# One gate-product step moved ahead of the score-value products, and their wait split in two

## The chip, the cores and the metric

The kernel runs on one core of one Trainium2 chip. The metric is the device time of the whole program in microseconds (us), all stages from the first load to the last store; lower is better. Every number below comes from the kernel before the change: three timed runs and one profiled execution.

## What is computed

One step of a hybrid decoder layer over 1024 prompt tokens and 8 x 4 sample tokens (1056 in all), model width 1024. The part that matters here is gated linear attention in chunks and the branch gates:

```
proj = rms_norm(x) @ w_in            # GLU input, q, k, v, output gate r, low-rank forget gate, gate_c, gate_g
# per chunk of tokens and head; b = cumulative log forget gate inside the chunk
o     = (q * exp(b)) @ s  +  att @ v          # att[t,s] = sum_k q[t,k] k[s,k] exp(b[t,k]-b[s,k]), s <= t
s_new = exp(b_last) * s   +  (k * exp(b_last - b)).T @ v
o     = rms_norm(o) * gla_norm * silu(r)
h     = x + (sigmoid(gate_c) * conv_out + sigmoid(gate_g) * (o @ w_gla_out)) @ w_out
out   = h + hierarchical_moe(rms_norm(h))     # 4 groups x 8 experts, top 2
```

Heads: 4, with 128 key and 256 value channels each.

## The kernel before, in words

The instruction stream of each engine is written out by hand, in the order in which it runs; engines wait for each other through counting semaphores (`wait_ge`, `then_inc`). The stages are: the input projection by slabs of 512 columns, with every weight and activation split into a high and a low part (three matmuls replace one); the causal convolution; **the chunk stage**; the sample tokens with the convolution's output product; the product with `w_gla_out`; `w_out` and routing; the experts; the last norm.

The chunk stage has 8 chunks of 128 tokens. In each, TensorE runs two independent kinds of work, interleaved by hand:

- **Gate products** (`gate_block`, L1148). Per chunk 2 column blocks of the gates (k = 0, 1) times 3 thirds of the tokens (j = 0 to 2). One product is 8 steps over the contraction (`parts`), and one step is three matmuls with 352 columns: `nTH,gateH`, `nTL,gateH`, `nTH,gateL`. All six have L999 as their line, the helper that records a matmul. Products (k, j) are numbered g = 3k + j and alternate between PSUM banks 0 and 1 (`bk[g % 2]`). Before the first step of a product TensorE waits until ScalarE has taken the product that was two numbers earlier (L1151). ScalarE takes a product by writing it to `stage` (`gate_out`).
- **The attention of the chunk** (`chunk`, L1158). First 9 "levels" (LV = 7): seven small products of decayed queries and keys (`gwork`), the diagonal product (`qkbuf`, l = 7), and the transposes of the decayed keys `kdT` (L1177, l = 8), each in bank 2 or 3. Behind each of the first eight levels stands one step of gate product (1, 0). VectorE takes each level out of PSUM: levels 0 to 7 are copied under masks into the scores `attn` (L2127, L2134), level 8 into the turned keys `kdn` (L2139). Each taking raises `lev_taken` by one; it starts at 2.
- Then come the **score-value products** (`vrbuf,attn` and `state,qe`, four heads, banks 4 and 5), which raise `o_ready`; then the **state products** (`vrbuf,kdn`, banks 6 and 7), which raise `ds_ready`; then gate products (1, 1) and (1, 2); a drain; and the transposes of the normed output `onorm` (L1204).

Beside this VectorE updates `state` after `ds_ready` (L2085), forms `onorm` (L2095), and prepares the next chunk (`prepare`, L1889). ScalarE squares the outputs after `o_ready`, takes gate product (1, 0), computes the exponentials of the next chunk (`factors`), and takes gate products (1, 1) and (1, 2) in the midst of those. SyncE loads the next chunk's inputs and gate columns when `oT_ready` and `gw_free` allow it, and after the last chunk the states and the weights of the convolution's output product (`cw_raw`). GpSimd only stores `stage` here.

The wait ahead of the score-value products stands at L1184: it asks for `lev_taken` to be `c * (LV + 2) + (LV + 4)`, which is all nine levels of the chunk, `kdn` among them.

Of the kernel before, what the change touches and what calls it, by code (L numbers as in the profile page):

```python
# [39 lines left out]
def hybrid_layer(nc, a, o):  # L40
# [13 lines left out]
    KC = D // P  # L54
# [5 lines left out]
    LV = 7  # L60
# [28 lines left out]
    with ctx:  # L89
# [3 lines left out]
        def sem(name):  # L93
            return ctx.enter_context(nc.semaphore(name))
# [208 lines left out]
        lev_taken = sem("lev_taken")  # L303
# [250 lines left out]
        def third(j):  # L554
            return slice(j * BLK, (j + 1) * BLK)
# [441 lines left out]
        def _(pe):  # L997
            def mm(out, lhsT, rhs, start, stop, **kw):
                return pe.matmul(out, lhsT=lhsT, rhs=rhs, start=start, stop=stop, **kw)  # L999
# [24 lines left out]
            def by_token(out, wh, wl, t0, parts=range(KC)):  # L1024
                for k in parts:
                    last = three(out, wh(k), wl(k), nTH[:, k, t0], nTL[:, k, t0], k == 0, k == KC - 1)
                return last
# [35 lines left out]
            for n in range(1, 1 + H + CC):  # L1063
# [4 lines left out]
                else:  # L1068
                    c = B_JOB.index(n)
# [37 lines left out]
            for m in range(VRJ):  # L1107
# [15 lines left out]
                if m in LN_JOB:  # L1123

                    j = LN_JOB.index(m)
# [9 lines left out]
                if m - 1 in LN_JOB:  # L1135

                    j = LN_JOB.index(m - 1)
# [10 lines left out]
            def gate_block(c, b, k, j, parts=range(KC)):  # L1148
                g = k * 3 + j
                if parts[0] == 0:  # L1150
                    pe.wait_ge(gate_taken, c * 6 + (g + 1))  # L1151
                    if j == 0:
                        pe.wait_ge(low_made, c * 2 + (N_SLAB + k + 1))
                last = by_token(bk[g % 2][:, 0:BLK], lambda q: gateH[k][:, q, :], lambda q: gateL[2 * b + k][:, q, :],
                                third(j), parts)
                if parts[-1] == KC - 1:
                    last.then_inc(gate_ready, 1)

            def chunk(c, b, i):
                for j in range(3):  # L1160
                    gate_block(c, b, 0, j)
                pe.wait_ge(prep_made, c + 1)
                lv = lev.rearrange("p l (h t) -> p l h t", h=H)
                for l in range(LV + 2):
                    x = (LV + 2) * b + l
                    pe.wait_ge(lev_taken, c * (LV + 2) + (l + 1))
                    dst = bk[2 + x % 2]
                    for h in range(H):
                        if l < LV:
                            m = 64 >> l  # L1170
                            right = lv[:, l, h, :].rearrange("p (n z i) -> p n z i", z=2, i=m)[:, :, 1, :]
                            last = mm(dst[:, 64 * h:64 * h + 64].rearrange("p (n i) -> p n i", i=m),
                                      lv[:, l, h, :], right, True, True)
                        elif l == LV:
                            last = mm(dst[:, P * h:P * h + P], qkb[b][:, 1, h, :], qkb[b][:, 0, h, :], True, True)
                        else:
                            last = pe.transpose(dst[:, P * h:P * h + P], kdT[:, h, :], ident[:, :])  # L1177
                    last.then_inc(lev_ready, 1)

                    if l < KC:  # L1180
                        gate_block(c, b, 1, 0, [l])

                pe.wait_ge(oT_taken, c + 1)
                pe.wait_ge(lev_taken, c * (LV + 2) + (LV + 4))  # L1184
                pe.wait_ge(s_made, c + 1)
                pe.wait_ge(vc_loaded[b], i * 16 + 16)
                for h in range(H):
                    dst = bk[4 + h // 2][:, DV * (h % 2):DV * (h % 2 + 1)]
                    mm(dst, attn[:, h, :], vch[b][:, h * DV:(h + 1) * DV], True, False)
                    last = mm(dst, qe[:, h, :], state[:, h, :], False, True)  # L1190
                last.then_inc(o_ready, 1)
                for h in range(H):
                    last = mm(bk[6 + h // 2][:, DV * (h % 2):DV * (h % 2 + 1)], kdn[:, h * P:(h + 1) * P],
                              vch[b][:, h * DV:(h + 1) * DV], True, True)
                last.then_inc(ds_ready, 1)
                for j in range(1, 3):
                    gate_block(c, b, 1, j)
                pe.drain().then_inc(gw_free, 1)
                o_transposes(P, c + 1)

            def o_transposes(r, wait):
                pe.wait_ge(on_made, wait)
                for k in range(KC):
                    last = pe.transpose(bk[4 + k // 4][:, P * (k % 4):P * (k % 4) + r],  # L1204
                                        onorm[0:r, k * P:(k + 1) * P], ident[0:r, 0:r])
                last.then_inc(oT_ready, 1)

            with pe.Fori(0, NCH // 2) as i:
                for b in range(2):
                    chunk(i * 2 + b, b, i)  # L1210
# [1286 lines left out]
```

## Time and profile before

| what | value |
|---|---|
| timed runs | 1838.51, 1838.77, 1839.8 us; median 1838.77 |
| profiled execution, own time | 1836.5 us |
| its span | 1834.9 us |
| mean granted TensorE clock | 0.97 of full speed |
| busy share of the span: TensorE, VectorE, ScalarE | 93%, 68%, 50% |
| HBM traffic | 324.35 MB read, 61.22 MB written |
| chunk stage (first gate product to last transposes) | about 470 to 780 us in the trace |

The profile gives busy time per engine, the chain of work that ended last, waits by who was waited for, and a timeline with the start of each instruction in us from the start of the span. PE is TensorE's matmul queue, PEld its weight loads, DVE VectorE, ACT ScalarE, POOL GpSimd, SP SyncE. Ends of matmuls are modelled and overlap the next start, so distances are best read from start to start.

### The profile page before, as it was taken

How to read it: one execution, taken by the hardware profiler on the slowest of the kernel's cores; microseconds unless marked ns; L12 is line 12 of the kernel's file. 1: busy time of each engine (PE TensorE's matmuls, PEld its weight loads, DVE VectorE, ACT ScalarE, POOL GpSimd, SP SyncE). 2: the span in 40 equal slices, each digit the busy share in tenths (PEclk: the TensorE clock that was granted, in tenths of full speed). 3: DMA queues.
4: the chain of work that ended last, by engine and by line, in shares of the span. 5: the costliest groups of instructions: out<-in, count | busy, mean ns of one | idle time of the engine just before them, and what ended most of it. 6: DMA issues, size and time to landing. Idle time of an engine off the chain costs nothing.

```text
span 1834.9 us, 24415 instructions
## 1 busy us (share of the span) xinstructions
PE 1710.3 (93%) x8996; PEld 1494.0 (81%) x8996; DVE 1239.1 (68%) x2000; ACT 913.8 (50%) x1085; POOL 226.4 (12%) x260
## 2 busy tenths in 40 slices
PE   6999989999899999989998996999999999999981
PEld 5999978777899999958997885788888888877771
DVE  5243789962566565653444556988989888888873
ACT  5262021114443333323433343787878877787763
POOL 3100111000000000001000123211111112221210
PEclk9999999999999999989999997999999999999995
DMA  4401222231124322153534327899999999999955
GB/s 172 139 36 59 70 93 100 88 107 38 65 87 137 123 86 86 43 197 98 183 120 161 104 88 264 321 360 376 364 384 383 383 392 388 377 375 376 359 204 194
DMA packets 101645, 366.18 MB, mean 200 GB/s; under 512 B 14389, under 2 KB 55569, under 8 KB 87744
## 3 DMA queue, kind: packets, MB, share of 16 engines
q1 hardware_dynamic: 78864, 308.06, 45.1%
q0 software_dynamic: 22704, 57.12, 9.7%
q8 instruction: 45, 0.74, 0.2%
q14 instruction: 32, 0.26, 0.0%
HBM read 324.35 MB, written 61.22 MB: 210 GB/s over the span
## 4 chain that ended last, share of the span: by engine, by line
PE 80%; DMA 6%; PEld 5%; DVE 4%; ACT 2%; issue 2%; DVEq 0%; PEldq 0%; SPq 0%; ACTq 0%; POOLq 0%
PE bank L999 77%; PEld bank L999 5%; DMA wraw_down<-in_w_expert_down 3%; PE bank L1401 2%; DMA wraw_gate<-in_w_expert_gate 1%; PE bank L1422 1%; DVE fbuf L2468 1%; DMA uo<-in_x_prompt 1%; DVE wL_gate L1889 0%; PE bank L1325 0%; PE bank L1204 0%; DMA stage<-xn_scr,kdT 0%; DMA h_scr<-ybuf,kdT 0%; DVE attn L2134 0%; DVE woL L1889 0%
## 5 line engine op out<-in xcount | busy, mean ns | idle before, releaser
L1889 DVE TENSOR_TENSOR wL_down<-wraw_down,wH_down 128x2048 fp32r<-128x2048 f32 x72 | 161.8, 2288 | 58.6 <-ACT wH_down L1490 58.6
L1889 DVE TENSOR_TENSOR wL_up<-wraw_up,wH_up 128x2048 fp32r<-128x2048 f32 x72 | 161.5, 2284 | 15.9 <-ACT wH_up L1490 15.9
L1889 DVE TENSOR_TENSOR wL_gate<-wraw_gate,wH_gate 128x2048 fp32r<-128x2048 f32 x72 | 161.6, 2286 | 6.3 <-ACT wH_gate L1490 6.1
L1490 ACT ACTIVATE wH_up<-wraw_up 128x2048 fp32r<-128x2048 f32 x72 | 134.1, 1910 | 59.2 <-DMA wraw_up<-in_w_expert_up 43.2
L1490 ACT ACTIVATE stage<-bank 128x512 f32<-128x512 f32 (+4 forms) x63 | 33.4, 546 | 255.3 <-PE bank L999 255.3
L2010 DVE SCALAR_TENSOR_TENSOR ybuf<-uo,gwork,ybuf 128x1024 f32<-128x1024 f32 x120 | 153.6, 1280 | 6.1 <-issue 6.1
L1490 ACT ACTIVATE wH_down<-wraw_down 128x2048 fp32r<-128x2048 f32 x72 | 133.8, 1910 | 12.8 <-DMA wraw_down<-in_w_expert_down 12.6
L999 PE MATMUL bank<-nTH,gateH 128*128 128x352 f32 x384 | 132.5, 345 | 5.3 <-DVE gateL L1889 5.3
L1490 ACT ACTIVATE wH_gate<-wraw_gate 128x2048 fp32r<-128x2048 f32 x72 | 134.2, 1923 | 2.6 <-DMA wraw_gate<-in_w_expert_gate 2.4
L999 PE MATMUL bank<-nTH,slabH 128*128 128x352 f32 x384 | 127.0, 331 | 5.9 <-DVE nTL L1889 5.6
L999 PE MATMUL bank<-nTL,slabH 128*128 128x352 f32 x384 | 124.9, 325 | 0.0
L999 PE MATMUL bank<-nTH,slabL 128*128 128x352 f32 x384 | 124.7, 325 | 0.0
L999 PE MATMUL bank<-nTL,gateH 128*128 128x352 f32 x384 | 124.2, 324 | 0.0
L999 PE MATMUL bank<-nTH,gateL 128*128 128x352 f32 x384 | 124.2, 323 | 0.0
L999 PE MATMUL bank<-wH_down,hidTH 128*128 128x512 f32 x288 | 113.7, 395 | 10.6 <-DVE hidTL L1889 10.6
L999 PE MATMUL bank<-slabH,nTH 128*128 128x512 f32 x288 | 116.8, 406 | 5.5 <-DVE slabL L1889 4.7
L943 POOL DMA_INDIRECT h_scr<-ybuf,kdT x36 | 67.5, 1875 | 433.6 <-ACT ybuf L1490 393.4
L999 PE MATMUL bank<-wH_gate,xeH 128*128 128x512 f32 x288 | 114.3, 397 | 6.4 <-DVE wL_gate L1889 3.8
L999 PE MATMUL bank<-wH_up,xeH 128*128 128x512 f32 x288 | 115.9, 402 | 0.0
L999 PE MATMUL bank<-slabH,nTL 128*128 128x512 f32 x288 | 114.3, 397 | 0.0
L999 PE MATMUL bank<-slabL,nTH 128*128 128x512 f32 x288 | 114.1, 396 | 0.0
L999 PE MATMUL bank<-wH_gate,xeL 128*128 128x512 f32 x288 | 113.5, 394 | 0.0
(309 smaller groups left out, 4297.2 us busy)
## 6 DMA issues: line engine op xcount, KB each, us to landing
wraw_gate<-in_w_expert_gate SPq DMA_DIRECT2D x36, 2048.0 KB, 14.9
wraw_up<-in_w_expert_up SPq DMA_DIRECT2D x36, 2048.0 KB
wraw_down<-in_w_expert_down SPq DMA_DIRECT2D x36, 2048.0 KB
slab_raw<-in_w_in SPq DMA_DIRECT2D x8, 2048.0 KB, 8.4
gate_scr<-stage POOLq DMA_DIRECT2D x16, 528.0 KB, 3.6
vr_scr<-stage POOLq DMA_DIRECT2D x32, 256.0 KB, 2.3
gate_raw<-in_w_in SPq DMA_DIRECT2D x16, 512.0 KB, 8.0
vrbuf<-vr_scr SPq DMA_DIRECT2D x16, 512.0 KB, 6.2
```

What stands on the lines that cost most here:

```text
L943: pool.indirect_dma_start(out=h_scr, in_=yo[n % 2], in_offset=None, out_offset=bass.IndirectOffsetOnAxis(ap=lst_tok[:, n:n + 1], axis=0), ...
L999: return pe.matmul(out, lhsT=lhsT, rhs=rhs, start=start, stop=stop, **kw)
L1401: last = pe.transpose(bk[k // 4][:, P * (k % 4):P * (k % 4 + 1)], xg[b][:, k:D:KC], ident[:, :])
L1422: last = pe.transpose(bk[4][:, P * k:P * (k + 1)], hid[:, k:DE:FC], ident[:, :])
L1490: return act.activation(out, in_, func, **kw)
L1889: return dve.tensor_tensor(out, x, y, op)
L2010: dve.scalar_tensor_tensor(ybuf[:, c, 0:SEQ], u[:, c, bass.ds(w, SEQ)], tap, ybuf[:, c, 0:SEQ], ALU.mult, ALU.add)
L2468: dve.scalar_tensor_tensor(fo[t][0:r, :], fh[t][0:r, :], rstd9[t][0:r, :], nfin[0:r, :], ALU.mult, ALU.mult).then_inc(f_made, 1)
```

## The change

In `chunk` of TensorE's program:

```diff
                     if l < KC:
                         gate_block(c, b, 1, 0, [l])
 
+                gate_block(c, b, 1, 1, [0])
                 pe.wait_ge(oT_taken, c + 1)
-                pe.wait_ge(lev_taken, c * (LV + 2) + (LV + 4))
+                pe.wait_ge(lev_taken, c * (LV + 2) + (LV + 3))
                 pe.wait_ge(s_made, c + 1)
                 pe.wait_ge(vc_loaded[b], i * 16 + 16)
                 for h in range(H):
@@
                 last.then_inc(o_ready, 1)
+                pe.wait_ge(lev_taken, c * (LV + 2) + (LV + 4))
                 for h in range(H):
                     last = mm(bk[6 + h // 2][:, DV * (h % 2):DV * (h % 2 + 1)], kdn[:, h * P:(h + 1) * P],
                               vch[b][:, h * DV:(h + 1) * DV], True, True)
                 last.then_inc(ds_ready, 1)
-                for j in range(1, 3):
-                    gate_block(c, b, 1, j)
+                gate_block(c, b, 1, 1, range(1, KC))
+                gate_block(c, b, 1, 2)
                 pe.drain().then_inc(gw_free, 1)
                 o_transposes(P, c + 1)
```

The score-value products now wait for eight levels, the state products for the ninth. The first step of gate product (1, 1) is issued ahead of both, the other seven remain behind them. No arithmetic changes, and no engine but TensorE has another order.

TensorE's order at the front of the score-value products, first chunk of the loop body; `kdT` is what the transposes read, `gateH_85` and `gateL_81` are the gate columns of block k = 1:

```order
 L1177 MATMUL bank<-ident,kdT 128x128 x4
-L1184 REGISTER_ALU
-L1186 ISA
+L1151 REGISTER_ALU
+L999 MATMUL bank<-nTH,gateH_85 128x352
+L999 MATMUL bank<-nTL,gateH_85 128x352
+L999 MATMUL bank<-nTH,gateL_81 128x352
+L1185 REGISTER_ALU
+L1187 ISA
 L999 MATMUL bank<-vrbuf,attn 128x256
```

Three matmuls now stand between the key transposes and the first score-value product, where there was only the wait.

The same engine behind the last score-value product; `kdn` is read by the state products:

```order
 L999 MATMUL bank<-state,qe 128x256
+L1193 REGISTER_ALU
 L999 MATMUL bank<-vrbuf,kdn 128x256 x4
-L1151 REGISTER_ALU
-L999 MATMUL bank<-nTH,gateH_85 128x352
-L999 MATMUL bank<-nTL,gateH_85 128x352
-L999 MATMUL bank<-nTH,gateL_81 128x352
```

A wait has come in ahead of the state products, and three of the 24 matmuls of gate product (1, 1) have left from behind them.

## Rows read from the trace of the kernel before

**Rows 1.** The page, busy time: us, share of the span, instructions.
```profile
PE 1710.3 (93%) x8996; PEld 1494.0 (81%) x8996; DVE 1239.1 (68%) x2000; ACT 913.8 (50%) x1085; POOL 226.4 (12%) x260
```
**Rows 2.** The page, chain that ended last, shares by engine.
```profile
PE 80%; DMA 6%; PEld 5%; DVE 4%; ACT 2%; issue 2%; DVEq 0%; PEldq 0%; SPq 0%; ACTq 0%; POOLq 0%
```
**Rows 3.** That chain in the chunk stage: start us, length us, what.
```profile
588.21 22.00 PE bank L999 x157
...
611.44 0.70 DVE kdn L2139
612.15 0.04 issue
612.19 13.15 PE bank L999 x72
...
650.55 0.12 issue
```
**Rows 4.** Waits of TensorE, 480 to 790 us: total us, times, longest.
```profile
PE bank L999 <- DVE kdn L2139: 9.1, 8, 1.2
```
**Rows 5.** Timeline, TensorE, end of one chunk's levels: start us, us, engine, line, what.
```profile
609.96 0.41 PE L999 MATMUL bank<-nTH,gateH 128*128 128x352 f32 x1
...
610.21 0.32 PE L999 MATMUL bank<-nTL,gateH 128*128 128x352 f32 x1
610.21 0.19 PEld L999 LDWEIGHTS bank<-nTH,gateL 128*128 128x128 f32 x1
...
610.36 0.32 PE L999 MATMUL bank<-nTH,gateL 128*128 128x352 f32 x1
...
610.52 0.60 PE L1177 MATMUL bank<-ident,kdT 128*128 128x128 f32 x4
...
612.19 0.70 PE L999 MATMUL bank<-vrbuf,attn 128*128 128x256 f32 x2 [1.07 <-DVE kdn L2139]
...
612.73 0.59 PE L999 MATMUL bank<-state,qe 128*128 128x256 f32 x2
...
613.16 0.59 PE L999 MATMUL bank<-vrbuf,attn 128*128 128x256 f32 x2
...
615.75 1.89 PE L999 MATMUL bank<-vrbuf,kdn 128*128 128x256 f32 x8
...
621.34 0.32 PE L999 MATMUL bank<-nTH,gateH 128*128 128x352 f32 x1
```
**Rows 6.** Timeline, VectorE, the same chunk: the last masked copy of the scores.
```profile
610.35 0.89 DVE L2134 COPY_PREDICATED attn<-masks,bank 128x128 f32<-128x128 int8 x4 [0.70 <-PE bank L999]
```
**Rows 7.** Timeline, TensorE, output transposes and the next chunk's first gate product.
```profile
625.45 1.09 PE L1204 MATMUL bank<-ident,onorm 128*128 128x128 f32 x8
...
626.30 0.41 PE L999 MATMUL bank<-nTH,gateH 128*128 128x352 f32 x1
```
**Rows 8.** Timeline, ScalarE, the same chunk: squares, gate products (1, 0) and (1, 1) taken.
```profile
615.95 0.38 ACT L1490 ACTIVATE gwork<-bank 128x256 f32<-128x256 f32 x1 [14.65 <-PE bank L999]
...
619.07 0.54 ACT L1490 ACTIVATE stage<-bank,par 128x352 f32<-128x352 f32 x1
...
624.93 0.54 ACT L1490 ACTIVATE stage<-bank,par 128x352 f32<-128x352 f32 x1
```
**Rows 9.** By stretch: us, busy PE, PEld, DVE, ACT, POOL, granted clock, DMA, GB/s.
```profile
610.00:648.30 38.30, 37.12 (x247) 35.96 (x246) 24.28 (x77) 14.36 (x28) 1.06 (x2) 1.00 0.33 104
...
795.00:800.00 5.00, 5.00 (x13) 2.43 (x13) 2.74 (x5) 3.40 (x7) 0.00 (x0) 0.50 0.42 97
...
1130.00:1500.00 370.00, 361.67 (x1697) 302.68 (x1698) 326.06 (x220) 292.88 (x244) 63.25 (x44) 0.98 0.97 368
```
**Rows 10.** Timeline behind the last chunk: last gate product taken (ScalarE), convolution weights issued (SyncE).
```profile
778.72 0.55 ACT L1490 ACTIVATE stage<-bank,par 128x352 f32<-128x352 f32 x1 [3.26 <-PE bank L999]
...
782.72 1.52 SPq L665 DMA_DIRECT2D cw_raw<-in_w_conv_out  x1
```
**Rows 11.** DMA issues, 470 to 800 us: KB each, us to landing.
```profile
cw_raw<-in_w_conv_out SPq DMA_DIRECT2D x1, 2048.0 KB, 13.8
```

## The prediction

> **What bounds the kernel now.** I began with the busy times: TensorE is at work 93% of the span, VectorE 68%, ScalarE 50% [rows 1]. The chain that ended last says the same: TensorE's matmuls make 80% of it [rows 2]. So what counts is time in which TensorE stands still, or work that it needn't do. The change touches the chunk stage alone, so I read the chain there [rows 3]. It is a plain alternation: 22.00 us of matmuls, then a hand-over through VectorE that ends in the copy of the turned keys (0.70 us) and an issue gap of 0.04 us (0.12 us in every second chunk), then 13.15 us of matmuls. The list of TensorE's waits gives the size of that hand-over: eight waits for the `kdn` copy, 9.1 us in all, 1.14 us each [rows 4]. Nothing else repeats in TensorE's waits there. The clock is granted in full in a whole chunk [rows 9], so matmul times can be taken as they stand.
>
> The timeline shows what the wait is for. The four key transposes start at 610.52; the first score-value product starts at 612.19 [rows 5]. Its operands `attn` were complete at 610.35 + 0.89 = 611.24 [rows 6]. What TensorE really stood for was the copy that ended at 611.44 + 0.70 = 612.14 [rows 3], and only the state products at 615.75 [rows 5] need that one.
>
> **The change part by part.**
>
> *The wait on the scores instead of the turned keys.* Between the start of the transposes and the first score-value product lie 612.19 - 610.52 = 1.67 us in this chunk, where the idle time is 1.07 us; with the mean idle of 1.14 us it is 1.74 us per chunk.
>
> *The step put in front.* When can it start? Eight transposes take 1.09 us and the next gate matmul starts 626.30 - 625.45 = 0.85 us after their start [rows 7]; four take 0.60 us [rows 5], 0.49 less, so the step should start 0.36 us after the transposes do. A step behind attention work lasts 610.52 - 609.96 = 0.56 us from start to start (0.25 + 0.15 + 0.16) [rows 5]. So the score-value products could start 0.36 + 0.56 = 0.92 us after the transposes, at 611.44 in this chunk. The scores are released at 611.24 plus the 0.04 to 0.12 us of issue [rows 3, 6], that is by 611.36. So the new wait is just covered by the moved step, with about 0.1 us to spare: front part 1.74 - 0.92 = **0.82 us saved** per chunk.
>
> *The step taken away from behind.* Three matmuls, 0.16 us from start to start each (the third in rows 5: 610.52 - 610.36), are gone from gate product (1, 1): **0.48 us saved**. The cold start behind the state products stays, it falls on the next step.
>
> *The start of the score-value products.* After the idle time the first group took 612.73 - 612.19 = 0.54 us, the next 613.16 - 612.73 = 0.43 [rows 5]. If weights are loaded ahead, 0.11 us goes too. Between 0 and 0.11 us; I count none of it, because TensorE can load ahead only in the 0.1 us by which the scores are early.
>
> *The second wait, ahead of the state products.* By the sum they start at about 611.44 + (615.75 - 612.19) = 615.0 [rows 5], and `kdn` is there at 612.14: 2.9 us of cover, cost nothing. What stands behind the wait on TensorE are the state products, for which VectorE waits, and the gate products. If that cover were gone, TensorE would wait for the rest of a 0.70 us copy.
>
> *The open group in bank 0.* Its first step needs gate product (0, 2) taken, which ScalarE did long before; SyncE's and GpSimd's queues are moved past nothing, and their issues follow TensorE's semaphores.
>
> Sum per chunk: 0.82 + 0.48 = 1.30 us, times 8 chunks = **10.4 us**. The bounds: 1.41 us with the start-up gained (11.3 us in all), and 1.14 us (9.1 us) if the weights of the first score-value product aren't loaded during the moved step: 0.16 us until its last matmul has ended, rather than started its successor.
>
> A rule of the Trainium skill prices the moved matmuls otherwise. The rows give 0.16 us from start to start for 352 columns. The page "TensorE: Matmul & The Clock Gate", section "Back-to-back issue gap", gives N/2.4 + 2.5 ns, which is 149 ns, an estimate, and no extra for following other work. By it the step costs 0.45 us in front and saves 0.45 us behind, 1.38 us per chunk and 11.0 us in all. I keep the rows' 0.56 and 0.48.
>
> **What is late next.** Everything downstream of the score-value products on VectorE and ScalarE moves up by 0.82 us, TensorE's own later work by 1.30 us, so all slacks against ScalarE shrink by 0.48 us. The nearest: the next chunk's first gate product uses bank 0 and needs product (1, 1) taken. Taken at 624.93 + 0.54 = 625.47 [rows 8], needed at 626.30 [rows 7]: 0.83 us of slack, 0.35 us left. Product (1, 0) was taken at 619.07 + 0.54 = 619.61 [rows 8] and is needed at 621.34 [rows 5]: 1.73, then 1.25 us. Both hold.
>
> **Does it reach the end?** The chunks' end releases all that follows: ScalarE takes the last gate product right behind TensorE [rows 10], and the convolution weights are issued only when the last chunk has freed their buffer and land 13.8 us later [rows 10, 11]. Loads with fixed durations therefore shift with the chunks. The profiled execution took 1836.5 us; the sum makes it 1826.1. It lies 2.3 us under the median of the timed runs, so I take the 10.4 us from the median: 1838.77 - 10.4 = **1828.4 us**, a ratio of 0.9943. A measurement of this kernel can tell about 0.2% from no change, 3.7 us.
>
> **The rivals.**
>
> *Weights aren't loaded ahead.* The trace shows the load of the next weights at 610.21 under a matmul that runs from 609.96 for 0.41 us [rows 5], which speaks against it. Price as worked out: 1.14 us per chunk, 9.1 us, 1829.7 us. The same page of the Trainium skill says in its Part 3, "What overlaps and what doesn't", that a weight load overlaps a running matmul only in another row group; here the row group is the same, and that row disagrees.
>
> *ScalarE becomes the next wait.* If the taking of product (1, 1) doesn't move up with `o_ready`, because its exponentials are held by something else, TensorE wants bank 0 at 626.30 - 1.30 = 625.00 and gets it at 625.47 + 0.1: 0.57 us lost at seven hand-overs, 4.0 us. The gain is 6.4 us: 1832.4 us. For it: the slack is only 0.35 us. Against it: squares, root, norm and differences all start from `o_ready` and `ds_ready`.
>
> *The gain is swallowed later.* In the expert stage the DMA engines are busy 0.97 of the time [rows 9]. If the stream of expert weights set the end and didn't start earlier, nothing would be left: 1838.8 us. Against it: the stream starts on buffers that TensorE's products free.
>
> *The clock turns it round.* After the last chunk TensorE idles and runs at half clock (0.50 in the stretch from 795 to 800 us, 1.2 instead of 2.4 GHz) until the convolution products have run for a while [rows 9]. Such stretches may fall otherwise when everything shifts. Work at full clock done at half clock costs its own duration again; if 15 us of the convolution or expert products fell into such a stretch anew, the loss is 15 us against the gain of 10.4: 1843.4 us. It decides the sign from 10.4 us of such work on. Against it: the stretch before is short, and the idle time that leads to it is the same after the change.
>
> *The change doesn't do what it says*: the scores may be released later than thought, so that the wait remains in part. Since the scores' copy ends 0.90 us before the keys' copy, at the very least the step behind and most of this are gained; the result is one of the times above.
>
> **How the numbers follow.** Forecast (9.8 to 11.3 us gained) 0.65; weights not ahead 0.12; ScalarE late 0.11; swallowed 0.05; clock 0.03. 0.04 is left for larger gains, where a stretch at half clock gets shorter by some us. The range for 8 in 10 reaches from 1825.5 (13 us gained) to 1832.8 (6 us gained), which takes in the first three cases with about 1 us of scatter, as the timed runs show. Faster by over 0.2%: 0.92; within 0.2%: 0.05; slower by over 0.2%: 0.03.
>
> **What would show it.** Right: in the chunk stage the eight waits for `kdn` are gone, the distance from the key transposes to the first score-value product is 0.9 to 1.0 us with three gate matmuls in it, and a chunk lasts 37.0 instead of 38.3 us. ScalarE's row of taking product (1, 1) ends 0.3 us before the next chunk's first gate matmul. Wrong: a wait of TensorE for `attn` at that place; a wait for `stage` on ScalarE ahead of a chunk's first gate product; or a chunk stage shorter by 10 us while the whole is not, with more time at clock 0.50 or a DMA row in the chain of the expert stage.

## The result, and the profile after

The changed kernel takes 1826.64 us in the median of five runs (1824.81 to 1829.32), the kernel before 1838.51 us in five (1835.01 to 1839.8). The medians lie 11.9 us apart, where 10.4 us were forecast. The ratio over all runs is 0.9942, with a 95% interval from 0.9931 to 0.9954; it isn't the quotient of the two medians (0.9935), and by it the gain is 10.7 us. The time lies inside the stated range.

The profiled execution of the changed kernel took 1824.81 us, its span is 1823.2 us, 11.7 us less than before. Where they went is seen from two groups of rows, the key transposes and the output transposes of the chunk stage. The view gives count, duration in ns (min/median/max) and the first and last start in us. Kernel before:

```profile
L1177 PE MATMUL bank<-ident,kdT x32: 270/272/273, 495.5 to 764.2; 128*128 128x128 f32 x32
```
```profile
L1204 PE MATMUL bank<-ident,onorm x64: 272/273/328, 510.5 to 779.5; 128*128 128x128 f32 x64
```

Changed kernel, the same two:

```profile
L1177 PE MATMUL bank<-ident,kdT x32: 271/273/273, 494.5 to 753.7; 128*128 128x128 f32 x32
```
```profile
L1206 PE MATMUL bank<-ident,onorm x64: 272/273/328, 508.1 to 767.7; 128*128 128x128 f32 x64
```

From the first key transpose to the last output transpose it was 779.5 - 495.5 = 284.0 us and is 767.7 - 494.5 = 273.2 us: **10.8 us** less. Another 1.0 us lies ahead of the chunk stage, which the change doesn't touch. Behind it nothing differs: 1834.9 - 779.5 = 1055.4 us and 1823.2 - 767.7 = 1055.5 us. The first and last key transposes span seven chunks plus 0.4 us within a group of four: (268.7 - 0.4)/7 = 38.3 us per chunk before, (259.2 - 0.4)/7 = 37.0 us after.

TensorE's waits of the changed kernel between 470 and 790 us no longer hold the eight waits of [rows 4]; the one for `kdn` that is left belongs to the sample tokens:

```profile
PE bank L999 <- DVE gateL L1891: 5.3, 1, 5.3
PE bank L999 <- DVE attn L2129: 4.2, 2, 3.1
PE bank L999 <- DVE kdT L1891: 3.0, 1, 3.0
PE bank L1233 <- DVE attn L2136: 1.1, 1, 1.1
PE bank L999 <- DVE kdn L2141: 0.9, 1, 0.9
```

The timeline of TensorE at the changed place (start us, length us, engine, line, operation, what) answers to [rows 5]:

```profile
605.37 0.60 PE L1177 MATMUL bank<-ident,kdT 128*128 128x128 f32 x4
605.73 0.41 PE L999 MATMUL bank<-nTH,gateH 128*128 128x352 f32 x1
605.97 0.32 PE L999 MATMUL bank<-nTL,gateH 128*128 128x352 f32 x1
606.13 0.33 PE L999 MATMUL bank<-nTH,gateL 128*128 128x352 f32 x1
606.29 0.59 PE L999 MATMUL bank<-vrbuf,attn 128*128 128x256 f32 x2
606.72 0.59 PE L999 MATMUL bank<-state,qe 128*128 128x256 f32 x2
```

And VectorE beside it, which answers to [rows 6]:

```profile
605.20 0.90 DVE L2136 COPY_PREDICATED attn<-masks,bank 128x128 f32<-128x128 int8 x4 [0.69 <-PE bank L999]
606.30 0.69 DVE L2141 COPY kdn<-bank 128x512 f32<-128x512 f32 x1 [0.20 <-issue]
```

The scores are complete at 606.10, the moved step ends its turn at 606.29, and TensorE goes straight on. The copy of the keys has only begun then; it ends at 606.99, long before the state products, which start at 609.74. In the chain that ended last, VectorE has vanished from this stage ([rows 3] had it in every chunk); one chunk of the changed kernel reads (start us, length us, what):

```profile
605.53 0.44 PE bank L1177 x4
605.97 12.82 PE bank L999 x72
618.79 0.11 issue
618.89 1.09 PE bank L1206 x8
619.99 22.47 PE bank L999 x160
```

### The profile page after: what moved, and what is told of

Same layout as the page of the kernel before. It is cut to its first block, busy times and chain, and to the rows that moved or that the text cites. A ratio compares the mean times of both kernels' runs of the same rounds, so it can differ in the third digit from the quotient of the medians.

```text
span 1823.2 us, 24423 instructions
## 1 busy us (share of the span) xinstructions
PE 1708.6 (94%) x8996; PEld 1493.9 (82%) x8996; DVE 1239.2 (68%) x2000; ACT 914.5 (50%) x1085; POOL 230.7 (13%) x260
## 4 chain that ended last, share of the span: by engine, by line
PE 82%; DMA 6%; PEld 5%; DVE 3%; ACT 2%; issue 1%; DVEq 0%; PEldq 0%; SPq 0%; ACTq 0%; POOLq 0%
PE bank L999 78%; PEld bank L999 5%; DMA wraw_down<-in_w_expert_down 3%; PE bank L1403 2%; DMA wraw_gate<-in_w_expert_gate 1%; PE bank L1424 1%; DVE fbuf L2470 1%; DMA uo<-in_x_prompt 1%; DVE wL_gate L1891 0%; PE bank L1327 0%; PE bank L1206 0%; DMA stage<-xn_scr,kdT 0%; DMA h_scr<-ybuf,kdT 0%; ACT wH_down L1492 0%; ACT ybuf L1492 0%
```

## The experiments

All experiments edit `chunk` of TensorE's program, or ScalarE's `factors`, and were measured in three groups. The first holds the changed kernel again, its two halves and the three steps in front; the second the earlier taking with three steps, the step ahead of the transposes and the first two versions without the drain; the third the change with the earlier taking, all three edits together, and the changed kernel once more. Diffs are against the changed kernel where nothing else is said. Each group has its own runs of the kernel before on the same chip; its median was 1836.22, 1837.74 and 1837.77 us. "A chunk" is worked out as above, from the first and last start of the key transposes in the profiled execution. Differences of a few tenths of a microsecond per chunk are read from these rows; the timed runs alone, which scatter by several microseconds, would not show them.

### The changed kernel again

No edit.

> The changed kernel once more, as the measure for the others of this group. My theory: 10.9 us under the kernel before (1.38 us in each of 8 chunks less small change), a chunk of 36.9 to 37.0 us, the first score-value product 0.92 us behind the start of the key transposes. Rival (part of the 11.9 us between the medians was scatter between runs): the ratio comes out above 0.9960, 7 us or less.

Measured: 1826.83 us, ratio 0.9950 (0.9937 to 0.9964), a chunk of 36.95 us, products 0.92 us behind the transposes. By the medians the gain is 9.4 us, between my 10.9 us and the rival's 7, so part of the 11.9 us was scatter. A third execution, in the last group:

> The changed kernel again, as the measure for this group. My theory: a chunk of 36.95 us, 10.9 us of gain in the chunk stage, and the rest of any difference between executions lies ahead of the chunk stage. Rival: the chunk stage itself differs between executions by 1 us or more.

Measured: 1828.81 us, ratio 0.9948 (0.9934 to 0.9961), a chunk of 37.0 us. From the first key transpose to the last output transpose the three executions took 273.2 us, 770.9 - 497.9 = 273.0 us and 769.0 - 495.6 = 273.4 us. So the chunk stage agrees within 0.4 us. The spans, 1823.2, 1826.9 and 1827.4 us, differ by up to 4.2 us: the second starts its chunk stage 3.4 us later, the third takes 3 us longer behind it. My expectation put all scatter ahead of the chunk stage; it also lies behind. Its cause stays open.

### Half of the change: the step alone

```diff
-                pe.wait_ge(lev_taken, c * (LV + 2) + (LV + 3))
+                pe.wait_ge(lev_taken, c * (LV + 2) + (LV + 4))
@@
-                pe.wait_ge(lev_taken, c * (LV + 2) + (LV + 4))
```

> The step is moved in front, but the score-value products wait for all nine levels as before. My theory: the step fits under the wait for the turned keys, the products start 1.67 to 1.82 us behind the transposes as before, and only the 0.47 us behind is gained: a chunk of 37.85 us, 3.8 to 4 us in all, and TensorE's waits for the kdn copy shrink to about 0.7 us each without vanishing. Rival (the moved step alone brings the gain, the wait was nearly over): a chunk below 37.2 us, 9 us or more in all.

Measured: 1832.58 us, ratio 0.9978 (0.9969 to 0.9987), 3.6 us between the medians; a chunk of (760.9 - 494.7 - 0.4)/7 = 38.0 us. Its timeline shows the step under the wait, and the products still 610.42 - 608.74 = 1.68 us behind the transposes:

```profile
608.74 0.60 PE L1177 MATMUL bank<-ident,kdT 128*128 128x128 f32 x4
609.10 0.41 PE L999 MATMUL bank<-nTH,gateH 128*128 128x352 f32 x1
...
610.42 0.70 PE L999 MATMUL bank<-vrbuf,attn 128*128 128x256 f32 x2 [0.60 <-DVE kdn L2140]
```

The rival, that the step alone does it, falls. The chunk is 0.1 us longer than I expected. The waits are as expected (6.2 us over nine); in four of the seven chunks TensorE's stretch from the first gate product to the next key transposes took 22.70 us instead of 22.55, with no wait in it. The extra time builds up in small amounts, most of it over the first 11 us of the stretch, so it isn't one stall. It happened in one, none and two chunks of the changed kernel's three executions, not in that of the kernel before, and stays unexplained.

### The other half: the wait alone

```diff
-                gate_block(c, b, 1, 1, [0])
@@
-                gate_block(c, b, 1, 1, range(1, KC))
+                gate_block(c, b, 1, 1)
```

> The wait is split, no step is moved. My theory: TensorE still idles between the key transposes and the scores, but only until the scores are released: products 0.76 to 0.9 us behind the start of the transposes, a chunk of 37.4 us, 7.2 to 7.8 us in all; the first group still takes 0.54 us. The two halves of the change then add up to 11 to 11.5 us. Rival (splitting alone does it all, the step adds nothing): a chunk of 37.0 us and 10.5 us or more.

Measured: 1830.19 us, ratio 0.9969 (0.9957 to 0.9981), 6.0 us between the medians; a chunk of (758.0 - 495.7 - 0.4)/7 = 37.4 us, which over eight chunks is 7.3 us. TensorE now waits for the scores, 1.7 us over eight times, and the first group takes 0.54 us again (609.22 - 608.68):

```profile
607.90 0.60 PE L1177 MATMUL bank<-ident,kdT 128*128 128x128 f32 x4
608.68 0.70 PE L999 MATMUL bank<-vrbuf,attn 128*128 128x256 f32 x2 [0.18 <-DVE attn L2135]
609.22 0.59 PE L999 MATMUL bank<-state,qe 128*128 128x256 f32 x2
```

The two halves come to 3.6 + 6.0 = 9.6 us by medians, the whole change in the same group to 1836.22 - 1826.83 = 9.4 us; I had expected 11 to 11.5 us. From the first key transpose to the last output transpose the halves save 284.0 - (775.8 - 494.7) = 2.9 us and 284.0 - (772.4 - 495.7) = 7.3 us, 10.2 us together; the step alone has four of the unexplained 0.15 us in it, which with one such stretch in the changed kernel makes up most of what is missing to 10.8 us. They add up: the split takes 0.9 us of wait away, the step takes 0.47 us of work from behind and fills what the split leaves open.

### More steps in front, no split

```diff
-                gate_block(c, b, 1, 1, [0])
+                gate_block(c, b, 1, 1, range(3))
                 pe.wait_ge(oT_taken, c + 1)
-                pe.wait_ge(lev_taken, c * (LV + 2) + (LV + 3))
+                pe.wait_ge(lev_taken, c * (LV + 2) + (LV + 4))
@@
-                pe.wait_ge(lev_taken, c * (LV + 2) + (LV + 4))
@@
-                gate_block(c, b, 1, 1, range(1, KC))
+                gate_block(c, b, 1, 1, range(3, KC))
```

> No split, but three steps (nine matmuls) in front, so that the wait for the turned keys is covered too: products 1.88 us behind the start of the transposes. TensorE's own sum is as good as the change's (a chunk of 36.95 us). My theory: ScalarE's taking of gate product (1,1) starts from the score-value products, comes 0.96 us later, and TensorE waits 0.7 us for bank 0 ahead of each next chunk: a chunk of 37.6 to 37.75 us, 5.5 to 6 us of gain. Rival (that slack isn't what it seems, ScalarE isn't next): a chunk of 36.9 to 37.0 us and the same time as the change.

Measured: 1830.62 us, ratio 0.9972 (0.9960 to 0.9984), 5.6 us; a chunk of (760.7 - 496.0 - 0.4)/7 = 37.8 us. The wait for the keys is covered, and a new one stands ahead of the next chunk's gate product. TensorE:

```profile
622.96 1.09 PE L1205 MATMUL bank<-ident,onorm 128*128 128x128 f32 x8
624.57 0.42 PE L999 MATMUL bank<-nTH,gateH 128*128 128x352 f32 x1 [0.52 <-ACT stage L1491]
```

ScalarE, where it takes gate product (1, 1):

```profile
623.90 0.54 ACT L1491 ACTIVATE stage<-bank,par 128x352 f32<-128x352 f32 x1
```

The chain that ended last shows where that taking gets its time from: from the state products through VectorE's state update, norm, low part of the gate weights and differences, then ScalarE:

```profile
609.99 6.63 PE bank L999 x33
...
616.65 1.57 DVE state L2086 x4
...
618.93 1.26 DVE onorm L2096 x3
620.18 1.13 DVE gateL L1890
621.32 1.08 DVE gwork L1890 x4
...
623.90 0.55 ACT stage L1491
624.45 0.12 issue
624.57 22.73 PE bank L999 x160
```

So filling the wait with more gate work wins only half: what delays the score-value products delays this chain. The last two rows also give the price of the hand-over, 0.12 us from the end of the taking to TensorE's next matmul.

### The same, with ScalarE taking the product earlier

```diff
-                    if l in (2, 5):
+                    if l in (1, 5):
```

> The kernel with three steps in front and no split, in which ScalarE takes gate product (1,1) behind its second exponential instead of its third. My theory (that taking held TensorE for 0.75 us per chunk there): it comes 0.5 to 0.65 us earlier, TensorE's gap ahead of the next chunk's first gate product shrinks from 1.6 to 0.95 to 1.1 us (0.85 is no wait), a chunk of 37.05 to 37.25 us, 4 us less than with the third. Rival (the gap has another cause, the gate weights' low part on VectorE or the drain): the gap stays at 1.6 us and the chunk at 37.75 us.

Measured: 1828.58 us, ratio 0.9945 (0.9932 to 0.9959), 9.2 us under the kernel before; a chunk of (756.3 - 496.1 - 0.4)/7 = 37.1 us. The gap to the next gate matmul fell from 1.61 to 621.91 - 620.97 = 0.94 us, and ScalarE's taking ends at 621.24 + 0.54 = 621.78, 0.13 us before it:

```profile
620.97 1.09 PE L1205 MATMUL bank<-ident,onorm 128*128 128x128 f32 x8
621.91 0.42 PE L999 MATMUL bank<-nTH,gateH 128*128 128x352 f32 x1
```
```profile
621.24 0.54 ACT L1491 ACTIVATE stage<-bank,par 128x352 f32<-128x352 f32 x1
```

That shows the cause of the new wait: moving nothing but this one taking by 0.7 us took nearly all of it away (0.85 us would be no wait at all). In the changed kernel itself the same edit should do nothing:

> The change, with gate product (1,1) taken behind the second exponential. My theory: in the change that taking ends 0.16 us before it would hold TensorE, so nothing changes: a chunk of 36.95 us and the time of the change. Rival (it already costs something): a chunk of 36.85 us or less.

Measured: 1828.33 us, ratio 0.9944 (0.9931 to 0.9956), beside 1828.81 us for the change in the same group; chunks without the unexplained 0.15 us last 36.92 to 36.96 us, as the change's do. The taking costs the change nothing.

### The step ahead of the key transposes

```diff
                     if l < KC:
                         gate_block(c, b, 1, 0, [l])
+                    if l == LV:
+                        gate_block(c, b, 1, 1, [0])
 
-                gate_block(c, b, 1, 1, [0])
```

> The change, but the moved step stands ahead of the key transposes instead of behind them. My theory: the scores are released 0.1 us before TensorE could use them, so the order of step and transposes hardly matters; the 0.09 us that a gate matmul loses behind attention work is saved: a chunk of 36.85 to 36.9 us, 0.5 to 0.7 us less than the change in all, no more than a measurement can tell. Rival (the transposes' later start makes VectorE's copy of the keys late for the state products, or the scores are late now): a wait of TensorE for attn or kdn in each chunk, a chunk of 37.0 us or more.

Measured: 1827.66 us, ratio 0.9938 (0.9925 to 0.9952), a chunk of (755.8 - 496.0 - 0.4)/7 = 37.1 us. This group has no run of the change itself, so the comparison goes by the chunk rows. Neither side was right. No wait for `attn` or `kdn` came up, but nothing was saved:

```profile
607.18 0.60 PE L1177 MATMUL bank<-ident,kdT 128*128 128x128 f32 x4
607.61 0.60 PE L999 MATMUL bank<-vrbuf,attn 128*128 128x256 f32 x2
```

Four transposes take 0.43 us ahead of a score-value product and 0.36 us ahead of a gate matmul; most of the 0.09 us saved at the step is lost again here. Two of the seven chunks last 36.96 us, as most of the change's do. The others are 0.07 to 0.19 us longer, because TensorE took 7.68 instead of 7.61 us from the first gate matmul behind the state products to the output transposes, or the 0.15 us of above, or both. Whether the moved step brings that on is open.

### Without the drain

```diff
-                pe.drain().then_inc(gw_free, 1)
-                o_transposes(P, c + 1)
+                o_transposes(P, c + 1, True)
 
-            def o_transposes(r, wait):
+            def o_transposes(r, wait, free=False):
@@
+                    if free and k == 0:
+                        last.then_inc(gw_free, 1)
                 last.then_inc(oT_ready, 1)
```

> The change, and the drain ahead of the output transposes is gone; the first output transpose raises gw_free instead. My theory: the gap from the last gate matmul to the first transpose shrinks from 0.42 to 0.16 us, a chunk of 36.7 us. The slack against ScalarE's taking of product (1,1), 0.28 us now, is then nearly used up but holds: 2.1 us less than the change in all, 12.9 us under the kernel before. Rival (ScalarE becomes the next wait, or the drain costs nothing): a chunk of 36.9 us and a gap moved to the next chunk's first gate product.

Measured: 1824.51 us, ratio 0.9933 (0.9919 to 0.9946), a chunk of (752.4 - 494.1 - 0.4)/7 = 36.8 us. The gap ahead of the output transposes shrank to 0.16 us, but the next gate matmul follows 618.94 - 618.02 = 0.92 us behind them instead of 0.85. ScalarE's taking ends at 618.27 + 0.54 = 618.81, and 0.12 us on is 618.93:

```profile
617.86 0.33 PE L999 MATMUL bank<-nTH,gateL 128*128 128x352 f32 x1
618.02 1.04 PE L1205 MATMUL bank<-ident,onorm 128*128 128x128 f32 x8
618.94 0.42 PE L999 MATMUL bank<-nTH,gateH 128*128 128x352 f32 x1
```
```profile
618.27 0.54 ACT L1493 ACTIVATE stage<-bank,par 128x352 f32<-128x352 f32 x1
```

About half of the expected 0.26 us per chunk arrived. In all seven hand-overs the gate matmul follows the end of the taking by 0.12 or 0.13 us: ScalarE had become the bound, as the rival had it, though the profile's list of waits names none. With the step ahead of the transposes as well:

> Step ahead of the transposes and no drain. My theory: TensorE alone would need 36.6 us per chunk, but the slack against ScalarE is 0.28 - 0.26 - 0.1, about -0.1 us: a wait of up to 0.1 us for stage ahead of each chunk, a chunk of 36.65 to 36.7 us, 2.0 to 2.7 us less than the change. Rival (both savings in full): 36.55 us and no wait for stage.

Measured: 1824.84 us, ratio 0.9932 (0.9918 to 0.9946), a chunk of 36.8 us, no better than without that move and longer than the 36.65 to 36.7 us that I expected. In all seven hand-overs the gate matmul again follows the end of ScalarE's taking by 0.12 or 0.13 us, so ScalarE holds this version too, and the rival's 36.55 us falls.

### Change, no drain, taken earlier

The edit of ScalarE's order above, on the kernel without the drain.

> The change without the drain, and ScalarE takes gate product (1,1) behind its second exponential. My theory: without the drain the chunk was held at 36.85 us by that taking, which TensorE sees 0.12 us after its end; 0.5 us earlier it holds nothing, the distance from the output transposes to the next gate matmul is back at 0.85 us, and a chunk lasts 36.68 to 36.75 us: 2.0 us less than the change in all, 13 us under the kernel before. Rival (something else held it, as the longer issue behind transposes without a drain): the distance stays at 0.92 us or more and the chunk at 36.85 us.

Measured: 1823.44 us (1822.86 to 1824.61), ratio 0.9919 (0.9907 to 0.9932); a chunk of (753.4 - 496.5 - 0.4)/7 = 36.6 us:

```profile
619.73 1.03 PE L1205 MATMUL bank<-ident,onorm 128*128 128x128 f32 x8
620.52 0.40 PE L999 MATMUL bank<-nTH,gateH 128*128 128x352 f32 x1
```

The distance is 0.79 us, so the taking had held the version without the drain. It is even under the 0.85 us that I took for "no wait". This is the fastest version of the study: by the chunk rows 256.9 us where the change has 259.0 to 259.4, some 2.3 us less, and 5.4 us less than the change by the medians of its group, part of which is the scatter outside the chunk stage.

## Why the prediction was right

**The bound.** It said that TensorE stands still once per chunk for a copy that its next products don't need, and nothing else repeats. The eight waits are gone, TensorE is busy 36.89 of 37.00 us of a chunk at full granted clock:

```profile
605.00:642.00 37.00, 36.89 (x247) 35.97 (x246) 24.29 (x77) 14.37 (x28) 1.07 (x2) 1.00 0.36 107
```

**The front part.** Step at 0.36 us, 0.56 us long, products at 0.92 us: measured 0.36, 0.56 and 0.92 us, in each chunk. The 149 ns per matmul that the prediction worked out from the Trainium skill ("TensorE: Matmul & The Clock Gate", section "Back-to-back issue gap") don't come out here: the step's starts lie 0.24, 0.16 and 0.16 us apart. The page gives its formula for an isolated matmul, not for a stream of weight loads and matmuls as this is. That the scores would be ready just before is right too: 606.10 plus issue against 606.29. Without the step the new wait costs 0.2 us per chunk, as the split alone shows.

**The part behind.** 0.48 us forecast; between the state products and the output transposes it was 0.47 us less.

**The start of the score-value products.** Here the sum was too careful. I counted nothing of the 0.11 us. The first group took 606.72 - 606.29 = 0.43 us instead of 0.54: gained whole in this chunk; in every second one it took 0.47 us, about half of the gain. The weight loads (PEld) show why. Kernel before, where load and product start together after the wait:

```profile
612.19 0.30 PEld L999 LDWEIGHTS bank<-vrbuf,attn 128*128 128x128 f32 x2 [1.31 <-DVE kdn L2139]
```

Changed kernel, this chunk and the one ahead of it:

```profile
606.15 0.33 PEld L999 LDWEIGHTS bank<-vrbuf,attn 128*128 128x128 f32 x2
```
```profile
569.26 0.30 PEld L999 LDWEIGHTS bank<-vrbuf,attn 128*128 128x128 f32 x2
569.33 0.64 PE L999 MATMUL bank<-vrbuf,attn 128*128 128x256 f32 x2
```

The load starts 0.05 us after the scores are complete (606.10) and 0.14 us before its product in the first case, and 0.12 us after them (569.14) and 0.07 us before its product in the second. So the gain hangs on how early the scores are released, as the prediction reasoned; the 0.1 us of lead that it counted as nothing was enough for half of the gain or all of it. Over eight chunks it comes to 0.66 us; with 0.15 us lost in the one unexplained longer stretch this is the difference between the 10.4 us of the sum and the 10.8 us of the chunk stage. The rival without loading ahead falls with the same rows: the loads run ahead, and the product starts 0.16 us behind the start of the last gate matmul, like any other.

**The whole.** The medians differ by 11.9 us, 1.1 us more than the chunk stage accounts for; in the two later groups it was 9.4 and 9.0 us. The chunk stage of the three profiled executions of the change agrees within 0.4 us, so I put the rest of these differences down to scatter outside it. That is argued, not shown: the kernel before was profiled only once. That a single median comes as near to the forecast time as this is partly luck.

**ScalarE next.** The forecast left 0.35 us of slack for the taking of gate product (1, 1) and gave its failure 0.11. Product taken at 618.92 + 0.54 = 619.46, gate matmul at 619.74: 0.28 us. The 0.83 us of before came from a chunk in which TensorE's gate products took 0.07 us longer than usual; five of the seven hand-overs had 0.76 us (the first: taken at 510.55, gate matmul at 511.31), and 0.76 - 0.48 is the 0.28 us found. The working also left out the 0.12 us until TensorE sees a taking, so only 0.16 us were really free. The argument was sound and the margin thinner than stated: 0.26 us more from TensorE used it up. The rows that show it:

```profile
618.92 0.54 ACT L1492 ACTIVATE stage<-bank,par 128x352 f32<-128x352 f32 x1
```
```profile
619.74 0.41 PE L999 MATMUL bank<-nTH,gateH 128*128 128x352 f32 x1
```

**Nothing swallowed, no turn of the clock.** The time behind the chunk stage is the same to 0.1 us in the first two profiled executions. The granted clock over the span is 0.969 after 0.970; in the 90 us behind the chunk stage (from 780 us before, from 768 us after) it is 0.91 in both, and 0.96 from there on in both. The agreement to 0.1 us is luck in part: over all thirteen profiled executions that time lies between 1054.7 and 1058.5 us, and the change's own three have 1055.5, 1056.0 and 1058.4 us. A loss of the whole gain is excluded by every group of timed runs; one of a microsecond or two behind the chunk stage is not.

## What to carry to other kernels

Look at what a wait for a counter asks for beyond what the next instruction reads: here one count too many cost 0.9 us per chunk. Independent work in front of the wait pays twice, by filling idle time and by shortening the work behind; but put there no more than the wait is long, because everything that the delayed products release moves back with them. When a saving shortens one engine's period, redo the slack against each other engine with the hand-over's own latency in it.

## What the runs showed of the hardware that I had not expected

- A drain between the last gate matmul and the transposes left 0.42 us from start to start where 0.16 us is the pace; without it the gap is 0.16 us, and the following transposes to the next gate matmul took 0.79 instead of 0.85 us once nothing held them.
- The same four transposes occupy 0.36 us ahead of a gate matmul and 0.43 us ahead of a score-value product, so the reordering tried here moved a small cost and removed next to nothing.
- In some chunks a stretch of 22.55 us of matmuls without any wait took 22.70 us. Several versions show it; its cause stays open.
- The weights of the first score-value product were loaded 0.05 or 0.12 us after the scores were complete, under the last gate matmul; a lead of 0.14 us over the product hid all 0.11 us of the start, one of 0.07 us about half.
